# A chunked recurrence: operands turned by whole-array transposes, the first level of the inverse masked and turned on VectorE, every product on its head's own half

## The reference, cut to what matters

```python
def step(S, inp):                       # S: (B, H, 64, 64)
    r_t, w_t, k_t, v_t, kk_t, a_t = inp
    sa = jnp.einsum('bhij,bhj->bhi', S, -kk_t)
    S = (S * w_t[:, :, None, :] + sa[..., None] * (kk_t * a_t)[:, :, None, :]
         + v_t[..., None] * k_t[:, :, None, :])
    return S, jnp.einsum('bhij,bhj->bhi', S, r_t)
_, ys = lax.scan(step, S0, xs)          # over 528 tokens
```

## Time and profile before

| | |
|---|---|
| median of 3 runs | 2566.52 us (2561.25 to 2567.20) |
| profiled execution | 2562.34 us, its span 2560.5 us |
| TensorE, weight loads | 2494.7 us, 2223.9 us busy |
| VectorE, ScalarE, GpSimd | 1194.6, 829.9, 124.5 us busy |
| recurrence on TensorE | 632.45 to 760.84 us |

### The profile page before, as it was taken

How to read it: one execution, slowest core, us unless ns; L and a number is a source line. 1 busy time by engine, 2 the same in 40 slices (tenths; PEclk the granted TensorE clock), 3 DMA queues, 4 the chain that set the end, 5 groups by cost and what they waited for, 6 DMA issues and landing times.

```text
span 2560.5 us, 44169 instructions
## 1 busy us (share of the span) xinstructions
PE 2494.7 (97%) x19506; PEld 2223.9 (87%) x19506; DVE 1194.6 (47%) x1795; ACT 829.9 (32%) x1326; POOL 124.5 (5%) x130
## 2 busy tenths in 40 slices
PE   7999999999889999999999999999989999999998
PEld 7999999996877888888999999899777888888887
DVE  5444334646655444443444433232976445444423
ACT  4222223334233322333222222212874233322221
POOL 1000000000321000011000000000000001000000
PEclk9999999999999999999999999999999999999999
DMA  4322232220002223233222233232212323232232
GB/s 155 99 83 96 86 91 94 75 86 9 5 12 73 90 94 99 84 94 96 89 92 91 85 91 100 75 93 71 57 53 74 95 91 107 91 99 91 88 98 70
DMA packets 72350, 212.70 MB, mean 83 GB/s; under 512 B 12796, under 2 KB 20028, under 8 KB 72032
## 3 DMA queue, kind: packets, MB, share of 16 engines
q1 hardware_dynamic: 70496, 209.03, 25.8%
q0 software_dynamic: 480, 0.73, 0.1%
q10 hardware_dynamic: 1184, 0.12, 0.0%
HBM read 207.61 MB, written 2.20 MB: 82 GB/s over the span
## 4 chain that ended last, share of the span: by engine, by line
PE 93%; DVE 3%; ACT 2%; issue 2%; DMA 0%; DVEq 0%; ACTq 0%
PE PS L635 80%; PE PS L1018 1%; PE PS L1017 1%; PE PS L1019 1%; PE PS L1553 1%; DVE P L2170 1%; PE PS L2107 1%; PE PS L1512 1%; PE PS L1388 1%; PE PS L1565 1%; PE PS L2083 0%; PE PS L2063 0%; PE PS L1533 0%; PE PS L1563 0%; PE PS L1609 0%
## 5 line engine op out<-in xcount | busy, mean ns | idle before, releaser
L635 PE MATMUL PS<-NHI,WH 128*128 128x264 f32 (+3 forms) x3072 | 801.6, 318 | 19.3 <-DMA CST<-in_consts 15.4
L635 PE MATMUL PS<-NLO,WH 128*128 128x264 f32 (+3 forms) x3072 | 798.2, 318 | 0.0
L635 PE MATMUL PS<-NHI,WL 128*128 128x264 f32 (+3 forms) x3072 | 795.6, 317 | 0.0
L697 DVE TENSOR_TENSOR WL<-WR,WH 128x1024 fp32r<-128x1024 f32 (+2 forms) x393 | 481.8, 1227 | 607.6 <-ACT WH L691 607.4
L691 ACT ACTIVATE WH<-WR 128x1024 fp32r<-128x1024 f32 (+2 forms) x393 | 397.1, 1011 | 759.3 <-PE PS L635 724.0
L635 PEld LDWEIGHTS PS<-NHI,WH 128*128 128x128 f32 x3072 | 505.7, 189 | 63.8 <-issue 17.0
L635 PEld LDWEIGHTS PS<-NLO,WH 128*128 128x128 f32 x3072 | 508.1, 189 | 40.0
L635 PEld LDWEIGHTS PS<-NHI,WL 128*128 128x128 f32 x3072 | 507.8, 189 | 39.0
L635 PE MATMUL PS<-HH,WL 128*128 128x264 f32 (+1 forms) x1034 | 273.2, 320 | 0.0
L635 PE MATMUL PS<-HH,WH 128*128 128x264 f32 (+1 forms) x1034 | 273.2, 320 | 0.0
L635 PE MATMUL PS<-HL,WH 128*128 128x264 f32 (+1 forms) x1034 | 272.9, 319 | 0.0
(11 more groups left out here) (374 smaller groups left out, 2359.8 us busy)
## 6 DMA issues: line engine op xcount, KB each, us to landing
WR<-in_ffn_gate SPq DMA_DIRECT2D x88, 512.0 KB, 3.4
WR<-in_ffn_up SPq DMA_DIRECT2D x88, 512.0 KB, 3.5
WR<-in_ffn_down SPq DMA_DIRECT2D x64, 512.0 KB, 3.5
WR<-in_ffn_down SPq DMA_DIRECT2D x32, 384.0 KB, 3.1
WR<-in_w_gate SPq DMA_DIRECT2D x24, 512.0 KB, 3.4
WR<-in_w_out SPq DMA_DIRECT2D x16, 512.0 KB, 3.5
WR<-in_in_rkv SPq DMA_DIRECT2D x12, 512.0 KB, 3.4
WR<-in_w_branch SPq DMA_DIRECT2D x24, 256.0 KB, 2.6
```

The source lines that it names most:

```text
L635: last = e.matmul(bank, left[:, cols], right[:, a:b] if right.shape[1] == L else right, start=(kt == 0 and left is wh and right is hi), st ...
L697: e.tensor_tensor(WL[:, i % NSPLIT, 0:w], WR[:, i % NR, 0:w], WH[:, i % NSPLIT, 0:w].bitcast(F32), ALU.subtract).then_inc(S["w_lo"], 1)
```

## The change

Three things are changed in the recurrence.

First, the products with the identity (L1533) become true transposes of 128 channels by 128 tokens, the chunk's own 64 and the next chunk's 64: 12 per chunk. Of each result one quarter is the first head of the pair for this chunk and another the second head for the next chunk; ScalarE copies them apart in six copies of 64 partitions, and BCV gets a fifth buffer. The first chunk's second heads have no chunk before them and are turned by 12 products as before.

Second, the first level of the inverse is no longer multiplied. Its U part is masked by VectorE out of the score bank nb, the identity is added, and its T part is made from U by a transpose on VectorE (32x32 blocks, and this level only couples neighbours).

Third, T and U and all that is multiplied with them now lie in each head's own half, so every product of the stage is straight; the other half u disappears. With the two_takes of the first level gone, TensorE waits for the attention's last copies (sb_pt, sb_copy) at the head of the stage instead of at k = 1.

```diff
+        def turned_out(c, g):
+            return "bcv", 2 + 6 * c + (2 * g + 2 if c < 8 else g + 1)
...
                 tus += 1
                 tu_at[c, 0] = tus
-                two_takes.append((("tus", c), ("t1", c + 1)))
-                chunk_takes += [(("tr", c, 0), ("bcv", 2 * c + 1)), (("tr", c, 1), ("bcv", 2 * c + 2))]
+                if c == 0:
+                    chunk_takes += [(("first", g), ("bcv", g + 1)) for g in range(2)]
+                chunk_takes += [(("tr", c, g), turned_out(c, g)) for g in range(3)]
             if k == 2:
                 chunk_takes.append((("xv", c), ("vh", c + 1)))
...
-        heads_in_turn = [(p, slice(HD * half, HD * half + HD), slice(HD - HD * half, 2 * HD - HD * half))
-                         for p in range(4) for half in range(2)]
+        heads_in_turn = [(p, slice(HD * half, HD * half + HD)) for p in range(4) for half in range(2)]
...
             q.wait_ge("cleared", 4)
             q.wait_ge("sb_keep", 24)
+            q.wait_ge("sb_pt", 32)
+            q.wait_ge("sb_copy", 4)
...
-                    bank, free = chunk_bank["tus", c]
-                    q.wait_ge("sb_pt", 32)
-                    q.wait_ge("sb_copy", 4)
-                    q.wait_ge(*free)
-                    for w in range(2):
-                        for p, f, u in heads_in_turn:
-                            left, right, o = (KAPPA, BETA, f) if w == 0 else (BETA, KAPPA, u)
-                            last = e.matmul(PS[o, bank + w, 64 * p:64 * p + 64], left[f, p, tok], right[f, p, tok],
-                                            start=p == 0, stop=True, skip_group_check=True)
-                    last.then_inc(S["fscored"], 1)
-                    for g, parts in enumerate(((BETA, CHI), (VV,))):
+                    if c == 0:
+                        for g, parts in enumerate(((BETA, CHI), (VV,))):
+                            bank, free = chunk_bank["first", g]
+                            q.wait_ge(*free)
+                            for w, src in enumerate(parts):
...
+                                    last = e.matmul(PS[HD:128, bank, at:at + 64], src[HD:128, p, tok],
+                                                    CST[HD:128, CHUNK["ident"]:CHUNK["ident"] + HD],
+                                                    start=p == w == 0, stop=True, skip_group_check=True)
+                            last.then_inc(S["turned"], 1)
+                    width = 2 * CH if c < 8 else CH
+                    for g, src in enumerate((BETA, CHI, VV)):
                         bank, free = chunk_bank["tr", c, g]
                         q.wait_ge(*free)
-                        for w, src in enumerate(parts):
-                            for p, f, u in heads_in_turn:
-                                at = 256 * w + 64 * p
-                                last = e.matmul(PS[f, bank, at:at + 64], src[f, p, tok],
-                                                CST[f, CHUNK["ident"]:CHUNK["ident"] + HD],
-                                                start=p == w == 0, stop=True, skip_group_check=True)
+                        for p in range(4):
+                            last = e.transpose(PS[0:width, bank, 128 * p:128 * p + 128],
+                                               src[:, p, CH * c:CH * c + width], cst("ident"))
                         last.then_inc(S["turned"], 1)
                 if k == 2:
...
+                    q.wait_ge(*turned_out(c, 2))
...
-                        last = e.matmul(PS[u, bank, 64 * p:64 * p + 64], XC[f, p, 0], BCV[f, 2, p], start=p == 0,
+                    for p, f in heads_in_turn:
+                        last = e.matmul(PS[f, bank, 64 * p:64 * p + 64], XC[f, p, 0], BCV[f, 2, p], start=p == 0,
...
-                        last = e.matmul(PS[u, bank, 64 * p:64 * p + 64], LT[f, p], TU[f, 0, p], start=p == 0,
+                    for p, f in heads_in_turn:
+                        last = e.matmul(PS[f, bank, 64 * p:64 * p + 64], LT[f, p], TU[f, 0, p], start=p == 0,
...
-                            e.matmul(PS[f, bank, 64 * p:64 * p + 64], TU[u, 1, p], PM[u, p], start=p == 0,
+                            e.matmul(PS[f, bank, 64 * p:64 * p + 64], TU[f, 1, p], PM[f, p], start=p == 0,
                                      stop=True, skip_group_check=True)
-                        last = e.matmul(PS[u, bank + 1, 64 * p:64 * p + 64], PM[u, p], TU[u, 1, p], start=p == 0,
+                        last = e.matmul(PS[f, bank + 1, 64 * p:64 * p + 64], PM[f, p], TU[f, 1, p], start=p == 0,
...
-                    for g in range(2):
-                        q.wait_ge("turned", 2 * c + g + 1)
+                    if c == 0:
+                        for g in range(2):
+                            q.wait_ge("turned", g + 1)
+                            at = BCV[HD:128, 2 * g:2 * g + 2 - g].rearrange("p w a n -> p (w a n)")
+                            e.activation(at, PS[HD:128, chunk_bank["first", g][0], 0:512 - 256 * g],
+                                         ACT.Copy).then_inc(S["bcv"], 1)
+                    for g in range(3):
+                        turned = four(chunk_bank["tr", c, g][0], 128)
+                        q.wait_ge("turned", 2 + 3 * c + g + 1)
                         q.wait_ge("updated", c - 3)
                         q.wait_ge("outs", c - 4)
-                        at = BCV[:, 2 * g:2 * g + 2 - g].rearrange("p w a n -> p (w a n)")
-                        e.activation(at, PS[:, chunk_bank["tr", c, g][0], 0:512 - 256 * g],
-                                     ACT.Copy).then_inc(S["bcv"], 1)
+                        e.activation(BCV[0:HD, g], turned[0:HD, :, 0:HD], ACT.Copy).then_inc(S["bcv"], 1)
+                        if c < 8:
+                            e.activation(chunk_turned[(c + 1) % 5][HD:128, g], turned[HD:128, :, HD:128],
+                                         ACT.Copy).then_inc(S["bcv"], 1)
...
+                    q.wait_ge("scored", 2 * c + 1)
+                    q.wait_ge("solved", c - 3)
+                    e.tensor_tensor(TU[:, 1], four(chunk_bank["nb", c][0], 128)[:, :, 0:CH], chunk_const("first_u"),
+                                    ALU.mult).then_inc(S["t1"], 1)
+                    q.wait_ge("t1", 2 * c + 1)
...
-                    q.wait_ge("fscored", c + 1)
-                    q.wait_ge("solved", c - 3)
-                    mask = CST[:, CHUNK["first_t"]:CHUNK["first_t"] + 2 * CH].rearrange("p (w n) -> p w n", w=2)
-                    bank = chunk_bank["tus", c][0]
-                    e.tensor_tensor(TU, PS[:, bank:bank + 2, 0:256].rearrange("p w (a n) -> p w a n", a=4),
-                                    mask.unsqueeze(2).broadcast_to([128, 2, 4, CH]), ALU.mult).then_inc(S["t1"], 1)
-                    q.wait_ge("t1", c + 1)
-                    ident = CST[:, CHUNK["ident"]:CHUNK["ident"] + CH].unsqueeze(1).broadcast_to([128, 8, CH])
-                    both = TU.rearrange("p w a n -> p (w a) n")
-                    e.tensor_tensor(both, both, ident, ALU.add).then_inc(S["tu"], 1)
+                    q.wait_ge("t1", 2 * c + 1)
+                    e.tensor_tensor(TU[:, 1], TU[:, 1], chunk_const("ident"), ALU.add).then_inc(S["t1"], 1)
+                    q.wait_ge("t1", 2 * c + 2)
+                    e.transpose(TU[:, 0].rearrange("p a n -> p (a n)"),
+                                TU[:, 1].rearrange("p a n -> p (a n)")).then_inc(S["tu"], 1)
```

More of the change, by code:

```diff
@@ L421, in chunk_home @@
             rest = [small[:, 256 * i:256 * i + 256].rearrange("p (a n) -> p a n", a=4) for i in range(3)]
-            chunk_homes.append((NB, XC, TU, BCV, *rest))
+            chunk_homes.append((NB, XC, TU, *rest))
+            chunk_turned.append(BCV)
             return at
@@ L1577, in pe_rwkv @@
                     q.wait_ge(*free)
-                    for p, f, u in heads_in_turn:
-                        last = e.matmul(PS[u, bank, 64 * p:64 * p + 64], KAPPA[f, p, tok], S0[f, p], start=p == 0,
+                    for p, f in heads_in_turn:
+                        last = e.matmul(PS[f, bank, 64 * p:64 * p + 64], KAPPA[f, p, tok], S0[f, p], start=p == 0,
                                         stop=True, skip_group_check=True)
@@ L1586, in pe_rwkv @@
                     q.wait_ge(*free)
-                    for p, f, u in heads_in_turn:
-                        last = e.matmul(PS[f, bank, 64 * p:64 * p + 64], TU[u, 1, p], RS[u, p], start=p == 0,
+                    for p, f in heads_in_turn:
+                        last = e.matmul(PS[f, bank, 64 * p:64 * p + 64], TU[f, 1, p], RS[f, p], start=p == 0,
                                         stop=True, skip_group_check=True)
```

29 lines of the change are left out of this document (17 added, 12 removed).

## The result

| | before | after |
|---|---|---|
| median | 2566.52 us (3 runs) | 2578.99 us (4 runs, 2575.55 to 2580.86) |
| profiled execution, span | 2562.34, 2560.5 us | 2578.80, 2576.8 us |
| recurrence on TensorE | 632.45 to 760.84, 128.4 us | 633.34 to 767.99, 134.65 us |

With all runs of before made beside it (median 2564.78) the ratio is 1.0049 [1.0034, 1.0064]. The change costs about half a per cent, 9 to 13 us; 2574 had been forecast, with a range of 2564 to 2588. Three executions of before, among them the profiled one of e11, took 4074 to 11722 us and are left out of every figure.

What follows compares the result with a forecast made beforehand. TensorE bounds the recurrence, with code loading limiting its records. Terms (+0.9, +2.7, +1.6, -0.5, +0.9, +2.6, +0.4) sum to +8.6 us, taking the profiled 2562.3 to 2570.9; forecast set at 2574 from the timed runs, range 2564 to 2588.

Steps and rivals of the forecast that it cites:

- Part 1: Recurrence products on each head's own half: corners 0.94 instead of 0.52 us, 15 us more; lost overlaps 1.1 a chunk.
- corner at the old pace: Rival: a corner's two products still run four at a time on its own half; 15 us less, 2559; chance 8%.
- order in the corner: Rival: four records in a row for one quadrant make a corner take up to 1.88 us; +34, 2600; chance 8%.
- Full chunk: TensorE's 64-token chunk when the stage is full: 14.94 us work, 15.15 with one gap, against 14.51; +2.6 for four.
- Code loading: TensorE in the recurrence gets no more than 127 records per 3.9 us; faster stretches end in a gap.
- Gaps stay: Rival: TensorE's issue gaps are not code loading and remain, 12.6 us on top; +19, 2585; chance 3%.
- Part 3: ScalarE's two copies per chunk become six of 0.46 us; chunks 0 to 3 change by +2.7, +1.6, -0.5, +0.9 us.
- Part 4: Entry of the recurrence: TensorE waits for the last attention copy before the scores, not after them; +0.9 us.
- Part 5: First level on VectorE, and GpSimd: 1.3 us of work for 1.45, nb and xc delayed 0.46 us; cost nothing.
- Emptying: Last 33.13 us of the recurrence: corners grow while gaps of code loading go; +0.4 us.
- The clock: Rival: a lower-clock stretch with each chunk's transposes, 1.4 us lost 9 times; +12, 2586; chance 4%.
- part 2: Transposes and first level, per chunk: products of some 1.9 us removed, 12 transposes of 1.65 us added; records 464 to 398.

Runs made afterwards that it cites:

- e11: The kernel before, run again with no edit: ratio 0.9996, median 2565.64 us.
- e1: The changed kernel, run again with no edit: ratio 1.0037 to before, median 2576.36 us, stage 134.42 us.
- e12: The kernel before with no edit, profiled a second time: stage 125.15 us, full chunks 14.03 us in the mean.
- e5: Changed kernel with the corners' T products writing the other head's half, values not the reference's: ratio 1.0004 to before, 2566.36 us, stage 123.34 us.
- e6: Before plus true transposes and the first level on VectorE, crossed quadrants and late wait kept: ratio 0.9989, 2561.82 us, stage 120.63 us.
- e9: Before plus true transposes, values turned and copied first, first level on VectorE from NB in SBUF, crossed quadrants kept: ratio 0.9963, 2557.35 us, stage 116.90 us.
- e4: Before without the corners' T products, values not the reference's: ratio 0.9946, 2551.20 us, stage 112.23 us.
- e10: Changed kernel with the waits for sb_pt and sb_copy back at k = 1: ratio 1.0034 to before, 2575.21 us, stage 134.61 us.
- e3: Before plus only the 12 true transposes, their six copies and the fifth buffer: ratio 0.9996, 2564.21 us, stage 124.85 us.
- e2: Before with only the crossed products moved to each head's own half: ratio 1.0033, 2575.29 us, stage 138.22 us.

## Why the prediction was right, step by step

Direction, mechanism and range held: 2578.99 and 2576.36 us against 2574 (2564 to 2588). The sum of +8.6 us stands against +7.1 (stage and entry, first pair of profiles), +10.2 (e1 against e12: 134.42 less 125.15, plus 0.96) and 9 us between the kernels at one mean clock. Part of this agreement is luck. The sum was built on one profile of before, whose stage was 128.40 us; beside e12's 125.15 the same 137 would have stood for +12. And the terms missed in both directions: 0.9 us too much for the full chunks, 1.0 in the filling, 0.55 too little in the emptying.

- **Part 1, own half** (+15 us of corners, +1.1 of overlaps in a chunk): right. The corner is 0.94 us as said; e5 gives 1.67 us a chunk for the corners alone; e6 against the changed kernel gives 14 us for all crossings. For the overlaps, a full chunk takes 13.24 us in e5, where only the T products cross, and 12.09 in e9, where all products do that crossed before, 1.15 less; the two differ in VectorE's work and in the order of the copies too, but TensorE waits for neither there. The rivals *corner at the old pace* and *order in the corner* are refuted by the same row: 0.94, neither 0.52 nor 1.88. (The second was mispriced: 34 us on top of 2574 is 2608, not 2600.)
- **Full chunk** (14.94 of work, 15.15 with a gap): 14.91 measured. Its terms: scores 1.74 (704.09 to 705.83), corners 0.94, 16-record steps 0.47, transposes 1.46 with 0.14 ahead of them (1.60, forecast 1.65). The short gap that had been added did not come. Over four chunks +1.6 us against the earlier trace rows instead of +2.6, and +3.5 against e12 (59.65 less 56.13).
- **Code loading** ("no more than 127 records per 3.9 us"): the mechanism holds, the figure does not. For it: the landings of the packets beside the gaps (e12), e4, and the issue waits that went from 12.6 to 0.4 us as the records became fewer and the rest longer; the queue of code moved 13 pieces from 670 to 728 us instead of 15. Against a fixed 3.9: the last full chunk of e12 had its 466 records in 13.24 us, 3.61 per 127, and one chunk of e4 3.72 (402 in 11.76). What sets the length of a gap in one execution is likely the time of the packet, as said there, but not shown. The Trainium skill (Runtime: NRT & Kernel Launch, Instruction fetch mechanics) says that crossing a block of code is mostly hidden; the changed kernel agrees (0.4 us of issue waits in the stage), before does not (10.1 and 12.6). *Gaps stay* is refuted.
- **Part 3, copies** (+2.7, +1.6, -0.5, +0.9): +2.4, +1.3, -0.7, +0.7 (9.04, 9.04, 10.57 and 12.27 less). The mis-sized term is the pitch of the copies, 0.46, taken from two copies of 128 partitions in a row; here they come 0.40 us apart:

```profile
638.93 0.38 ACT L1640 ACTIVATE BCV<-PS 64x256 f32<-64x256 f32 x1
639.34 0.38 ACT L1642 ACTIVATE BCV<-PS 64x256 f32<-64x256 f32 x1
...
639.77 0.68 PE L1551 MATMUL PS<-BCV,XC 64*64 64x64 f32 x16 [1.61 <-ACT BCV L1642]
```

  L1551 starts 6.43 us after the scores (6.8 forecast), behind the sixth copy. In full chunks the copies are hidden, as said.
- **Part 4, the moved wait** (+0.9): 0.89 us of idle at the entry, and 0.96 by e10.
- **Part 5, VectorE**: the unknown transpose has 445 ns (0.42 taken). The addition of 128x256 was put at 0.42 and takes 845 ns in the mean, from 643 in chunk 0 to 946 in the full chunks:

```profile
L1679 DVE TENSOR_TENSOR TU<-TU,CST 128x256 f32<-128x256 f32 x9 | 7.6, 845 | 0.0
...
L1681 DVE STREAM_TRANSPOSE TU<-TU 128x256 f32<-128x256 f32 x9 | 4.0, 445 | 0.3
```

  All nine lie beside GpSimd's masking. In e9, where the addition moved by a step, seven of nine take 0.42 or 0.43 us; the two that start while a masked product of GpSimd is under way take 0.84 (VectorE's two rows, then GpSimd's):

```profile
665.75 0.84 DVE L1682 TENSOR_TENSOR TU<-TU,CST 128x256 f32<-128x256 f32 x1
678.35 0.43 DVE L1682 TENSOR_TENSOR TU<-TU,CST 128x256 f32<-128x256 f32 x1
...
664.70 1.60 POOL L1727 TENSOR_TENSOR TMP<-NB,CST 128x256 f32<-128x256 f32 x2
```

  In the full chunks it cost nothing: VectorE is busy for 9.1 of 14.91 us, and TensorE is never idle. In the filling this was not tested by itself.
- **Emptying** (+0.4): +0.95 (34.08 less 33.13), the one term too small. It is not shown which of its twelve rounds were off.
- **The clock**: the rival (a fall with every chunk's transposes) did not come; all windows of the stage are at 1.00, with 12 transposes in each full chunk. The Trainium skill (TensorE: Matmul & The Clock Gate, Part 4: PE-mode transpose) says that transposes don't count as activity; between other products, as they stand here, it makes no difference that a row shows. The one fall inside a stage (e5, at 643.45 us) came behind two waits of TensorE, 1.60 and 0.48 us; the changed kernel has the same waits at this place in three profiles and no fall, so the transposes are not shown to be its cause. What the prediction had no term for is that the clock of the rest of the kernel differs between executions by as much as the change is worth: e1's fastest and slowest runs are 2570.16 us at 0.995 and 2580.65 at 0.990.

The balance that the prediction drew is the one that the runs show: the gain of part 2 and of the vanished gaps against part 1. Both sides are there: e3 and e6 show the one side (-0.3 to -3.6 us for the first, -4.5 to -7.8 for both, in the stage), e2 the other (+9.8 to +13.1). The change bundles a gain with a larger loss, and e9 is the gain without it. The prediction had the loss in its terms but did not ask what the change would be worth without it.

## What to carry to other kernels

On small matrices count two things of a step, the quadrants it keeps busy and the records it issues; a product in a quadrant that would be idle costs next to nothing in the array (0.52 us for 32 records against 0.47 for 16), and moving it to its neighbour's quadrant costs 0.42 more. When a change bundles several edits, sum each by itself: here whole-array transposes and the first level on VectorE were worth keeping, the own halves not. An operation put first on another engine delays what stands behind it there, and so whoever waits for the bank that this frees: 0.58 us a chunk went this way in e6 and came back in e9.

## What was not expected of the hardware

- The same program's stage varied by 3.25 us between two profiles at the full clock (128.40, 125.15), through gaps of different length on the same records; the changed kernel, without such gaps, repeats within 0.23 us. The gaps end 1.2 to 1.5 us after a packet of 16 KB of code has landed.
- Copies of 64 partitions on ScalarE take 378 ns, those of 128 partitions 384 (L1651): half the partitions save nothing in the copy, but these came 0.40 us apart, not the 0.46 taken.
- An addition of 128x256 in SBUF on VectorE takes 0.42 us alone and 0.84 when it starts under a product of GpSimd, the rows of e9 above; one that starts ahead of GpSimd's product (655.88 and 656.07 us) keeps its 0.43, and GpSimd's takes 0.83 instead of 0.73. An addition that reads PSUM keeps its time (all nine of L1692 take 0.42, the one at 686.31 us beside GpSimd's product of 686.29 too), and so does the transpose, with one input in SBUF (445 ns in all nine, eight of them beside GpSimd's). The Trainium skill (SBUF — State Buffer, Who interferes with whom) says that a VectorE instruction with two inputs in SBUF contends with a GpSimd instruction that reads SBUF, and one with a single input there does not; all three agree.
- Before's run times follow the mean granted clock with 2.05 us for each 0.001, from 0.988 to 0.996.
